# A hybrid decoder step on one core: another order at the opening, and the first expert's selection moved into the routing block

## What is computed

```
h = rmsnorm(x, norm_mix);  u, zc, gb, gc = split(h @ w_in, 4)        # w_in 1024 x 2048
y_ssm = glu(gelu(diagonal_state_scan(u)))                              # 512 wide
y_conv = gb * conv3(gc * zc)                                           # 512 wide
x = x + concat(rmsnorm(y_ssm), rmsnorm(y_conv)) @ w_out
hf = rmsnorm(x, norm_ffn)
top_v, top_i = top_k(hf @ w_router + b_router, 4);  g = softmax(top_v) # 32 experts
x = x + sum over the 4 experts e of g_e * (swiglu(hf @ w_gate_up[e] + b) @ w_down[e] + b_down[e])
y = rmsnorm(x, norm_final)
```

## Time and profile before

| | |
|---|---|
| time, median of 3 runs | 1466.92 us (1466.55 to 1467.43) |
| the profiled execution's own time | 1467.44 us |
| its span, first to last instruction | 1465.5 us |
| PE busy | 1419.3 us, 97% of the span |
| DVE busy | 1320.9 us, 90% |
| ACT busy | 1031.1 us, 70% |
| POOL busy | 142.1 us, 10% |
| moved by DMA | 469.42 MB, 320 GB/s in the mean |

### The profile page before, as it was taken

The page is one execution under the profiler, slowest core; times in us unless marked ns, Lnnn a source line. Parts: engine busy times, 40 slices in busy tenths (PEclk is TensorE's granted clock), DMA queues, the critical chain, the costliest instruction groups (busy, mean ns, idle before and its releaser), DMA issues.

```text
span 1465.5 us, 22683 instructions
## 1 busy us (share of the span) xinstructions
PE 1419.3 (97%) x7043; PEld 1134.9 (77%) x7044; DVE 1320.9 (90%) x1755; ACT 1031.1 (70%) x1244; POOL 142.1 (10%) x151
## 2 busy tenths in 40 slices
PE   6999999899999999999999999999999999999992
PEld 5888844588888888888888888888888888888882
DVE  4887576899999999999999999999999999999994
ACT  4011432788878888888888888888888887888783
POOL 8100020100000000000000001000000010000000
PEclk9999999799999999999999999999999999999996
DMA  9510572799999999999999999998999999999953
GB/s 308 70 34 1 197 281 115 239 403 383 381 382 375 376 377 368 373 373 376 370 373 374 371 375 375 362 357 356 366 378 375 382 382 372 370 375 372 371 223 122
DMA packets 85286, 469.42 MB, mean 320 GB/s; under 512 B 17935, under 2 KB 19207, under 8 KB 68361
## 3 DMA queue, kind: packets, MB, share of 16 engines
q1 hardware_dynamic: 73160, 447.86, 76.3%
q0 software_dynamic: 12096, 21.18, 6.3%
HBM read 457.56 MB, written 27.82 MB: 331 GB/s over the span
## 4 chain that ended last, share of the span: by engine, by line
PE 80%; DMA 1%; DVE 1%; ACT 0%; issue 0%; SPq 0%; POOLq 0%
PE bank L1856 75%; PE bank L1847 2%; PE bank L1841 2%; PE bank L1863 1%; DMA token_sums<-ymix,row_cur 0%; DMA x<-token_sums 0%; PE bank L1834 0%; DVE x L2006 0%; DVE ymix L2006 0%; ACT ymix L1791 0%; ACT ring_lo L1815 0%; SPq L1692 0%; DVE ssf L71 0%; DVE ssf L69 0%; DVE ssf L68 0%
## 5 line engine op out<-in xcount | busy, mean ns | idle before, releaser
L1925 DVE TENSOR_TENSOR w_lo<-ring_lo,w_hi 128x1024 fp32r<-128x1024 f32 x527 | 610.0, 1220 | 22.5 <-ACT w_hi L1753 22.4
L1753 ACT ACTIVATE w_hi<-ring_lo 128x1024 fp32r<-128x1024 f32 x527 | 544.2, 1058 | 84.9 <-PE bank L1856 80.7
L1856 PE MATMUL bank<-w_hi,x_hi 128*128 128x512 f32 x1056 | 332.7, 396 | 0.0
L1856 PE MATMUL bank<-w_lo,x_hi 128*128 128x512 f32 x1056 | 326.6, 391 | 0.0
L1856 PE MATMUL bank<-w_hi,x_lo 128*128 128x512 f32 x1056 | 326.4, 390 | 0.0
L1925 DVE TENSOR_TENSOR w_lo<-w_out,w_hi 128x1024 fp32r<-128x1024 f32 x264 | 311.2, 1221 | 11.8 <-ACT w_hi L1753 11.8
L1753 ACT ACTIVATE w_hi<-w_out 128x1024 fp32r<-128x1024 f32 x264 | 268.3, 1055 | 18.5 <-PE bank L1856 18.5
L1856 PEld LDWEIGHTS bank<-w_lo,x_hi 128*128 128x128 f32 x1056 | 198.9, 188 | 42.1
L1856 PEld LDWEIGHTS bank<-w_hi,x_lo 128*128 128x128 f32 x1056 | 198.8, 188 | 42.0
L1856 PEld LDWEIGHTS bank<-w_hi,x_hi 128*128 128x128 f32 x1056 | 194.0, 189 | 37.0 <-issue 0.4
L1856 PE MATMUL bank<-w_hi,h_hi 128*128 128x512 f32 x528 | 169.9, 403 | 0.0
(11 more groups left out here) (365 smaller groups left out, 1175.4 us busy)
## 6 DMA issues: line engine op xcount, KB each, us to landing
ring_lo<-in_w_gate_up SPq DMA_DIRECT2D x132, 2048.0 KB, 11.7
w_out<-in_w_down SPq DMA_DIRECT2D x132, 1024.0 KB, 13.9
ring_lo<-in_w_in SPq DMA_DIRECT2D x4, 2048.0 KB, 22.2
w_out<-in_w_out SPq DMA_DIRECT2D x2, 2048.0 KB, 9.0
x<-in_x_prompt SPq DMA_DIRECT2D x6, 512.0 KB, 9.7
bias<-bias_rows SPq DMA_DIRECT2D x132, 3.0 KB
token_sums<-x SPq DMA_DIRECT2D x4, 512.0 KB
ffn_in<-hf SPq DMA_DIRECT2D x4, 512.0 KB, 6.6
```

The source lines that it names most:

```text
L1753: nc.scalar.activation(high(j), raw(j), ACT.Copy).then_inc(s["w_hi"], 1)
L1856: last = nc.tensor.matmul(bank[b + u][:], v[:, k, :], part(j)[:, u, :], start=(j == 16 and first), stop=(j in (7, 15, UNITS - 1) and part ...
L1925: v.tensor_tensor(low(j), raw(j), high(j).bitcast(F32), ALU.subtract).then_inc(s["w_lo"], 1)
```

## The change

At the opening, the first root is for tiles 0 and 1, the second for tile 2 alone, the third for tiles 3 and 4. The first 256 columns of w_in (1 MB of the 8) stand in SP's queue behind the third tile, under a semaphore of their own. norm_mix has its own semaphore, and its eight rows are transposed alone; three products of 512 columns whose result is not used follow on PE; the other rows of `prow` are transposed behind the third tile. The low parts of projections 0 and 1 run ahead of the high parts, and tiles 3 and 4 are transposed between them. The four loads of B go behind POOL's other loads and its memsets.

In the router, the root of tile q = 1 moves ahead of the first tile's expert choice. At its end, the count of tokens per expert moves ahead of the one-hot selection; the three parts of the last tile's gates are formed after the first step of the overflow tables; bias products 8 and 9 stand next to each other; the selection of expert 0 and its bias products move from the expert block into the router block; the gathered rows are transposed into banks 4 and 7, without waiting for bias products 0 and 1 to be copied out of their banks; ACT splits the first weight unit ahead of the last two bias copies. Two semaphores are those of the mixer, counted on.

```diff
-    FIRST = ((0, 3), (3, NT))
+    FIRST = ((0, 2), (2, 3), (3, NT))
...
-        for i in range(NT):
+        w_src = a["w_in"][0].rearrange("(k p) (b n) -> b p k n", p=P, b=4)
+        for i in range(3):
             load_x(i, x_in[i])
-        w_src = a["w_in"][0].rearrange("(k p) (b n) -> b p k n", p=P, b=4)
-        for blk in (0, 1, 3, 2):
+        sp.dma_start(w_in[:, 0, :, 0:2 * P], w_src[0][:, :, 0:2 * P]).then_inc(w_first, 16)
+        for i in range(3, NT):
+            load_x(i, x_in[i])
+        sp.dma_start(w_in[:, 0, :, 2 * P:4 * P], w_src[0][:, :, 2 * P:4 * P]).then_inc(w_in_in[0], 16)
+        for blk in (1, 3, 2):
...
-            act.wait_ge(s["rstd"], 1 if i < FIRST[0][1] else 2)
+            act.wait_ge(s["rstd"], 1 + sum(i >= hi for lo, hi in FIRST))
             nc.scalar.activation(xs[i][0:n], x[0:n, i, :], ACT.Copy, scale=ss[0:n, NT + i:NT + i + 1]).then_inc(s["xs"], 1)
 
         act.wait_ge(s["ones"], 1)
-        for i in range(3):
-            square(i)
+        square(0)
+        square(1)
         root(0)
+        square(2)
+        root(1)
+        scale(0)
+        scale(2)
         square(3)
         square(4)
-        root(1)
-        for i in (0, 2, 3, 4):
-            scale(i)
+        root(2)
+        scale(3)
+        scale(4)
...
-        pool.dma_start(prow[NM:NM + 8, :], a["norm_mix"][0].rearrange("(k p) -> k p", p=P)).then_inc(s["prow_in"], 16)
+        pool.dma_start(prow[NM:NM + 8, :], a["norm_mix"][0].rearrange("(k p) -> k p", p=P)).then_inc(norm_in, 16)
...
-        for r, n in enumerate(("ssm_b_re", "ssm_b_im")):
-            for g2 in range(2):
-                pool.dma_start(bt[g2 * NS:(g2 + 1) * NS, r], a[n][0].rearrange("(g a) n h -> a n g h", a=2)[g2]).then_inc(s["b_in"], 16)
...
+        for r, n in enumerate(("ssm_b_re", "ssm_b_im")):
+            for g2 in range(2):
+                pool.dma_start(bt[g2 * NS:(g2 + 1) * NS, r], a[n][0].rearrange("(g a) n h -> a n g h", a=2)[g2]).then_inc(s["b_in"], 16)
...
-        pe.wait_ge(s["prow_in"], 16 * 7)
-        nc.tensor.transpose(bank[0][:, 0:PC], prow[:], ident[0:PC, 0:PC]).then_inc(s["prow_psum"], 1)
+        pe.wait_ge(norm_in, 16)
+        nc.tensor.transpose(bank[0][:, 0:KD], prow[0:KD, :], ident[0:KD, 0:KD]).then_inc(s["prow_psum"], 1)
+        pe.wait_ge(x_in[0], 32)
+        for q in range(3):
+            nc.tensor.matmul(bank[7][:], ident[:], x[:, 0, 0:512], start=True, stop=True)
...
-        for p in range(NT):
+        for p in range(3):
             x_transposes(p)
+        pe.wait_ge(s["prow_in"], 16 * 6)
+        nc.tensor.transpose(bank[1][:, 0:PC], prow[:], ident[0:PC, 0:PC]).then_inc(s["prow_psum"], 1)
...
-            pe.wait_ge(w_in_in[m // 4], 16)
             if n >= 2:
+                pe.wait_ge(w_in_in[m // 4], 16)
                 taken(pe, n - 2)
             if n == 0:
-                pe.wait_ge(s["hT"], 2 * FIRST[0][1])
+                pe.wait_ge(w_first, 16)
+                pe.wait_ge(s["hT"], 2 * 3)
+                for n1 in range(2):
+                    for k in range(KD):
+                        nc.tensor.matmul(bank[2 * n1][:, 0:HALF], w_k(ORDER[n1], k), hT[:, k, 0:HALF], start=(k == 0), stop=(k == KD - 1))
+                    if n1 == 0:
+                        for p in range(3, NT):
+                            x_transposes(p)
+                pe.wait_ge(s["hT"], 2 * NT)
+            if n <= 1:
                 for k in range(KD):
-                    nc.tensor.matmul(bank[0][:, 0:HALF], w_k(m, k), hT[:, k, 0:HALF], start=(k == 0), stop=(k == KD - 1))
-                pe.wait_ge(s["hT"], 2 * NT)
-                for k in range(KD):
-                    last = nc.tensor.matmul(bank[1][:, 0:REST], w_k(m, k), hT[:, k, HALF:TOK], start=(k == 0), stop=(k == KD - 1))
+                    last = nc.tensor.matmul(bank[2 * n + 1][:, 0:REST], w_k(m, k), hT[:, k, HALF:TOK], start=(k == 0), stop=(k == KD - 1))
...
+        variance(0)
+        inverse(0)
+        dve.wait_ge(s["rstd"], 1)
+        ts(xs[1], x[:, 1, :], ss[:, NT + 1:NT + 2], ALU.mult).then_inc(s["xs_dve"], 1)
         dve.wait_ge(s["prow_psum"], 1)
-        nc.vector.tensor_copy(pcol[:], bank[0][:, 0:PC]).then_inc(s["pcol"], 1)
+        nc.vector.tensor_copy(pcol[:, 0:KD], bank[0][:, 0:KD]).then_inc(s["pcol"], 1)
         dve.wait_ge(s["pcol"], 1)
-        for p in range(NT):
-            take_hT(p)
+        variance(1)
+        inverse(1)
+        take_hT(0)
+        take_hT(1)
+        take_hT(2)
+        dve.wait_ge(s["prow_psum"], 2)
+        nc.vector.tensor_copy(pcol[:, KD:PC], bank[1][:, KD:PC]).then_inc(s["pcol"], 1)
+        variance(2)
+        inverse(2)
+        take_hT(3)
+        take_hT(4)
...
+    BD_BANK = [1, 2, 3, 4, 5, 0, 1, 2, 3, 5]
+    BD_AFTER = {6: 1, 7: 2, 9: 5}
+    XT_BANK = (4, 7)
...
         take_strips(0)
+        root(1)
         expo(0)
         spread(0)
-        root(1)
...
-        for j in range(5, 2 * NT):
+        for j in range(5, 2 * Q):
             take_bias(j)
         act.wait_ge(keep["landed"][0], 16)
         nc.scalar.activation(tb["w_hi0"][:, 0, :].rearrange("p (u n) -> p u n", u=2), unit0, ACT.Copy).then_inc(e["w_hi"], 1)
+        for j in range(2 * Q, 2 * NT):
+            take_bias(j)
...
         ranks(Q)
+        for j in range(NT):
+            last = nc.tensor.matmul(bank[6][0:E, 240:241], mask_b[:, j, :], ones_b[:, 0:1], start=(j == 0), stop=(j == NT - 1))
+        last.then_inc(s["count_psum"], 1)
         pe.wait_ge(e["onehot"], 1)
         for i in range(NT):
             last = nc.tensor.matmul(bank[6][:, 200:203], onehot[:, i, :], tb["slotval"][:, i, 0, 0, :], start=(i == 0), stop=(i == NT - 1))
         last.then_inc(s["first_psum"], 1)
         for j in range(4, 2 * Q):
             bias_rows(j)
-        for j in range(NT):
-            last = nc.tensor.matmul(bank[7][0:E, NT * E:NT * E + 1], mask_b[:, j, :], ones_b[:, 0:1], start=(j == 0), stop=(j == NT - 1))
-        last.then_inc(s["count_psum"], 1)
         pe.wait_ge(s["gate4"], NT)
         pe.wait_ge(keep["bd_sb"], 3)
         nc.tensor.transpose(bank[3][:, 0:P], gate4[:, Q].rearrange("p c e -> p (c e)"), ident[:]).then_inc(s["gT_psum"], 1)
-        pe.wait_ge(s["gT"], 2)
-        bias_rows(2 * Q)
         pe.wait_ge(s["extra"], 1)
         nc.tensor.matmul(bank[7][0:E, NT * E + 1:NT * E + 2], tri[0:E, 0:E], extra_b[:], start=True, stop=True).then_inc(s["upto_psum"], 1)
-        bias_rows(2 * Q + 1)
+        pe.wait_ge(s["gT"], 2)
+        for j in range(2 * Q, 2 * NT):
+            bias_rows(j)
         pe.wait_ge(s["passed"], 1)
         nc.tensor.matmul(bank[6][:, 256:256 + NB], ones_b[0:E, :], passed[:], start=True, stop=True)
-        nc.tensor.matmul(bank[6][:, 256 + NB:256 + 2 * NB], extra_b[:].to_broadcast([E, P]), passed[:], start=True, stop=True).then_inc(s["over_psum"], 1)
+        nc.tensor.matmul(bank[6][:, 256 + NB:256 + 2 * NB], extra_b[:].to_broadcast([E, P]), passed[:], start=True, stop=True)
+        for i in range(NT):
+            last = nc.tensor.matmul(bank[6][:, 208:214], onehot[:, i, :], tb["slotval"][:, i, 0, :, :].rearrange("p b c -> p (b c)"),
+                                    start=(i == 0), stop=(i == NT - 1))
+        last.then_inc(e["sel_psum"], 1)
         pe.wait_ge(e["x_in"], 16)
-        pe.wait_ge(keep["bd_sb"], 7)
         for h in range(2):
             for k in range(4 * h, 4 * h + 4):
-                last = nc.tensor.transpose(bank[h][:, (k % 4) * P:(k % 4 + 1) * P], xg[:, k * P:(k + 1) * P], ident[:])
+                last = nc.tensor.transpose(bank[XT_BANK[h]][:, (k % 4) * P:(k % 4 + 1) * P], xg[:, k * P:(k + 1) * P], ident[:])
             last.then_inc(s["gT_psum"] if h == 0 else e["xT_psum"], 1)
+        pe.wait_ge(keep["bd_sb"], 9)
+        pe.wait_ge(bias_in, bias_in0 + 64)
+        for c, b in enumerate((0, 2, 1, 3)):
+            last = nc.tensor.matmul(bank[b][:], tb["one_b"][32 * c:32 * c + 3, 0:1].to_broadcast([3, P]),
+                                    tb["bias"][32 * c:32 * c + 3, :], start=True, stop=False)
+        last.then_inc(e["bias_used"], 1)
...
+        def gate_parts(q):
+            i = TILES[q]
...
-            done(v.tensor_copy(count[:], bank[7][0:E, NT * E:NT * E + 1]))
+            done(v.tensor_copy(count[:], bank[6][0:E, 240:241]))
             done(v.tensor_scalar(tiles_in[:], nth[0:E, 1:NT], float(P), count[:, 0:1], ALU.mult, ALU.is_lt))
             done(v.tensor_reduce(extra[:], tiles_in[:], AX_X, ALU.add))
             v.tensor_copy(extra_b[:], extra[:]).then_inc(s["extra"], 1)
+            gate_parts(Q)
             dve.wait_ge(s["upto_psum"], 1)
             done(v.tensor_tensor(upto[:], bank[7][0:E, NT * E + 1:NT * E + 2], extra[:], ALU.add))
             v.tensor_scalar(passed[:], nth[0:E, 0:NB], upto[:, 0:1], -0.5, ALU.subtract, ALU.is_gt).then_inc(s["passed"], 1)
-            dve.wait_ge(s["over_psum"], 1)
+            dve.wait_ge(e["sel_psum"], 1)
...
         normed(0)
+        variance(1)
         pick_experts(0)
```

(20 more changed lines are left out.)

28 lines of the change are left out of this document (14 added, 14 removed).

## The result

| | before | after |
|---|---|---|
| median, runs on the same chips (20 each) | 1467.7 us (1465.72 to 1470.74) | 1470.29 us (1465.7 to 1472.63) |
| ratio to before | | 1.0016, 95% interval 1.001 to 1.0022 |
| profiled execution, its span | 1467.44, 1465.5 | 1472.06, 1470.3 |

The change made the kernel 2.6 us slower by the medians; 4.3 faster was forecast. The spread of after is the wider one: its fastest run is as fast as the fastest of before. The profiled execution of after, at 1472.06, is the third slowest of its 20, so that its trace shows a loss of 4.8 where the medians show 2.6.

What follows compares the result with a forecast made beforehand. PE was taken to bound the kernel, the expert loop running at its pace; 1.0 + 0.5 + 2.05 + 0.75 = 4.3 us off the profiled 1467.44 gave 1463.1, and 1462.6 as median; range 1460.3 to 1465.4.

Steps and rivals of the forecast that it cites:

- The step that failed: Expert loop: runs at PE's pace with no late weight, so an earlier first product makes the end earlier by as much.
- the third, slower: Opening: B's loads, last on POOL, land too late for their multiplication; 1468.1 if landing at 53; chance 0.04.
- Boundary and router's end, 2.05 + 0.75: Gathered rows transposed and split 2.05 us earlier; selection and bias products gone from the loop's boundary, 0.75.
- Second tile, 0.5: Router's second tile: PE's wait of 1.33 goes, DVE's chain is late next, so 0.5 us counted.
- Opening, 1.0: First projection: low part starts at 16.8 instead of 19.61, tile transpositions then take 1.6; 1.0 us kept.
- the 4.2 us behind PE's first work: Opening: PE's clock put to rise 4.2 us after its first work at 7.1, so at 11.3.
- The clock in the loop, 0 taken: Lower clock after the loop's first product: between 0.4 us lost and 1.4 won, counted as 0.
- the first rival: Loop: clock rises early, 3.1 us after the first product; 1.4 us more gain, 1461.2; chance 0.15.

Runs made afterwards that it cites:

- e4: Changed kernel without POOL's five transfers that add the biases' sums to token_sums (the adds): 1463.45 us, ratio 0.997.
- e9: Changed kernel, SP issuing expert 1's gate and up weights only once the first four of POOL's five adds into token_sums have landed: 1463.88 us, ratio 0.9975.
- e11: Changed kernel, SP issuing expert 1's gate and up weights only once three of POOL's five adds into token_sums have landed: 1463.53 us, ratio 0.9973.
- e2: Kernel before with the changed kernel's mixer, so the new opening alone: 1466.75 us, ratio 0.9993.
- e12: Changed kernel, expert 1's weights held until three adds have landed, plus two unused products in PE's gap at the opening: 1463.29 us, ratio 0.9969.
- e5: Changed kernel with POOL's five adds into token_sums issued in the router block, behind expert 0's gather: 1477.8 us, ratio 1.0069.
- e6: Kernel before with POOL's five adds into token_sums issued in the router block, behind expert 0's gather: 1479.78 us, ratio 1.0082.
- e7: Changed kernel with expert 1's weights and biases held back on SP until all five adds into token_sums have landed: 1467.12 us, ratio 0.9998.

## Why the prediction was wrong

**The step that failed** is the one ahead of the sum: "the expert loop runs at PE's pace from its first product to its last, no weight is late there, and whatever makes the first product ... earlier makes the end earlier by as much". It was argued from PE having no other wait. A wait of zero shows no slack: in the kernel before the gather for expert 1 landed at 302.0 and was used at 304.17, and 3.75 of pull (of coming earlier) was put on a slack of 2.2. Had the gather moved by 3.75 as PE did, it would have been in time. Had it moved by its issue's 2.7 alone, it would have landed at 299.3, in time too for PE at 300.42. But its own way was no constant: it became 6.1 longer, as the adds ahead of it ran beside the weights. The runs show this in its place: PE stood 5.04 for the gather and lost 2.5 more at the lower clock, and with the adds gone (e4) or the weights held (e9, e11) the wait is gone too. None of my rivals had it; the third, slower, was about the loads of B, and no run shows them late.

**Boundary and router's end, 2.05 + 0.75**: 2.4 measured (3.1 less the 0.7 that was there before the last tile). Products 8 and 9 overlap, as said. Most of the missing 0.4 is at the boundary: PE starts 0.65 behind DVE's end (269.12 to 269.77), where I took the 0.33 of before.

**Second tile, 0.5**: the wait of 1.33 is gone, 0.74 at the next transposition stands in its place (forecast 0.9), and 0.7 is left at 253.15, 0.1 of it the opening's.

**Opening, 1.0**: 0.1 in the changed kernel's profiled execution, 0.9 in that of e2. The forecast of the places was good (low part 16.8; 16.16 and 17.03 measured), that of the parameters' transposition too (29.6; 30.47). Missing was the gap of 1.93 ahead of the low part as a place where the clock can fall. The six instructions of the three products took 4.72 here, so that by the durations the clock rose near 10.7, and 5.49 in e4, all at the lower level, so that it rose not before 11.9, with PE's first work at 6.5 in both: the 4.2 us behind PE's first work that I counted with are no fixed time. The Trainium skill ("TensorE: Matmul & The Clock Gate", section "What's actually happening") has the recent activity set the clock; these runs agree so far as both the rise and the fall shift between executions of the same instructions.

**The clock in the loop, 0 taken**: it rose 3.6 after the first product, as the first rival had it (3.1), and gave the 1.1 that separates 3.1 at the first product from 4.2 at unit 8. DVE's splits did not hold PE, which had been my reason against that rival.

**Sum**: with the adds out of the way (e4) or the weights held (e11, e12) the change is worth 4.3, 3.9 and 4.0 us in the medians against the kernel before of the same chips. The terms were right to half a us together, and part of that is luck: at the loop's first product they had given 3.1 of 4.3, and the clock's 1.1, taken at 0, made up for it. The transfer that the loop's head waits for was not in the sum.

What the two queues do to each other has a rule that I had not used: the Trainium skill ("DMA: Bandwidth & Descriptors", section "Queues, rings and completion order") says that each DMA engine takes turns between the queues that have work for it. The runs agree with such sharing, though none shows the turns: the longer the weights stay away, the sooner the adds are done. Counted from the issue of the `w_down` loads, the last add landed after 33.4 us where the weights were issued 16.0 behind them (after), 29.3 where 18.1 (before), 27.1 where 19.7 (e11) and 22.6 where 22.3 (e9).

## What to carry to other kernels

Before saying that an earlier start makes an earlier end, look up for each transfer used after the moved part when it was issued, when it landed and when it was wanted; the smallest such slack bounds what is kept, and absence of a wait says nothing about it. A pull (what comes earlier) moves the issues of different engines by different amounts, so ask which transfers now run side by side that did not before. Where bulk loads are wanted late and a small transfer early, holding the bulk for a few us can be worth more than any order within a queue.

## What the runs showed of the hardware that I had not expected

- A block's end did not come until the accumulating transfers issued by POOL in it had landed (14.9 and 13.8 us of wait in e5 and e6; inferred from these two kernels), while loads of 1 MB issued by SP in the same block crossed it (landed at 282.4, end at 272.1, in the kernel before).
- The gather's 4.3 us with no weight load beside it (e7) becomes 11.1 to 11.7 beside weight loads and 17.4 behind a late add; in e9 the 4.2 MB of `w_down` and the 2.2 MB of adds, with nothing else of size beside them, took 22.6 us, some 280 GB/s, where weight loads alone move 420 to 430.
- A wait of 5 us inside the loop cost 7.5: PE's clock was at its lower level until 5.5 us after PE had restarted.
